# A gated delta-rule trunk: 512-column projections with a kept convolution edge, and the first tap on ScalarE

## The reference

```python
xn = rmsnorm(h, norm_g)
proj = xn @ w_in                                   # q, k, v, z (1024 columns each), two gate logits per head
qkv = silu(causal_depthwise_conv(proj[..., :3072], conv_w))   # 4 taps along the sequence, each channel by itself
q, k = l2norm(q) * 128 ** -0.5, l2norm(k)          # per head, 128 wide
o = chunked_delta_rule(q, k, v, beta, g)           # meta tokens as one chunk, the rest in chunks
h = h + (rmsnorm(o) * silu(z)) @ w_out
```

## Time and profile before

| | |
|---|---|
| median of three runs | 2801.99 us (2800.05 to 2802.21) |
| the profiled execution | 2798.55 us |
| its span, first to last instruction | 2796.6 us |
| mean granted TensorE clock | 0.958 |
| busy share: PE, DVE, ACT, POOL | 89%, 60%, 41%, 17% |
| `gated_deltanet` | from about 119 to about 1602 us |

### The profile page before, as it was taken

How to read it: one execution, slowest core, us unless ns; L and a number is a source line. 1 busy time by engine, 2 the same in 40 slices (tenths; PEclk the granted TensorE clock), 3 DMA queues, 4 the chain that set the end, 5 groups by cost and what they waited for, 6 DMA issues and landing times. The chain is left out here.

```text
span 2796.6 us, 50391 instructions
## 1 busy us (share of the span) xinstructions
PE 2498.3 (89%) x17193; PEld 2193.1 (78%) x17193; DVE 1671.3 (60%) x3872; ACT 1132.8 (41%) x3326; POOL 481.3 (17%) x377
## 2 busy tenths in 40 slices
PE   5568887899999999999999699999996999999997
PEld 4467777789998999999999468878885777777775
DVE  4367676777777777777777333333332666666664
ACT  4244454544444444444444244433331333333332
POOL 0144343310000000000000012100001333223331
PEclk9689999999999999999999689999997999999998
DMA  6664354544445444344453167743455222222221
GB/s 194 200 245 143 137 167 147 180 132 130 143 138 189 137 145 131 126 156 134 122 164 97 27 196 257 243 158 139 182 199 229 68 68 84 84 68 75 68 69 47
DMA packets 273813, 392.78 MB, mean 140 GB/s; under 512 B 79282, under 2 KB 187906, under 8 KB 273442
## 3 DMA queue, kind: packets, MB, share of 16 engines
q1 hardware_dynamic: 240066, 370.05, 39.6%
q10 hardware_dynamic: 33632, 21.26, 2.6%
HBM read 267.92 MB, written 123.31 MB: 140 GB/s over the span
## 5 line engine op out<-in xcount | busy, mean ns | idle before, releaser
L1227 PE MATMUL p_psp<-xg,p_whi 128*128 128x264 f32 x4096 | 842.4, 295 | 26.6 <-POOL p_wlo L1176 17.2
L1227 PEld LDWEIGHTS p_psp<-xg,p_whi 128*128 128x128 f32 x4096 | 655.5, 191 | 31.2 <-issue 21.9
L1227 PE MATMUL p_psp<-xg,p_wlo 128*128 128x264 f32 x2048 | 606.9, 296 | 0.0
L1227 PEld LDWEIGHTS p_psp<-xg,p_wlo 128*128 128x128 f32 x2048 | 391.6, 191 | 0.0
L981 DVE SCALAR_TENSOR_TENSOR p_acc<-p_proj,p_taps,p_acc 128x528 f32<-128x528 f32 x288 | 251.8, 874 | 5.4
L1822 PE MATMUL first_q<-first_w,p_o 128*128 128x512 f32 (+1 forms) x864 | 208.3, 401 | 17.0 <-DVE first_w L1786 17.0
L2364 PE MATMUL first_q<-first_w,p_hT 128*128 128x512 f32 x720 | 196.4, 413 | 13.4 <-DVE p_q L2250 13.0
L1822 PEld LDWEIGHTS first_q<-first_w,p_o 128*128 128x128 f32 (+1 forms) x864 | 157.4, 184 | 61.2 <-issue 17.0
L2364 PE MATMUL p_pso<-p_wo,p_oT 128*128 128x512 f32 x768 | 194.3, 404 | 7.9 <-DVE p_oT L2276 4.2
L862 ACT ACTIVATE p_sig<-p_sig 128x528 f32<-128x528 f32 x128 | 82.5, 645 | 293.1 <-DVE p_sig L983 293.1
L2364 PEld LDWEIGHTS p_pso<-p_wo,p_oT 128*128 128x128 f32 x768 | 143.7, 192 | 48.5 <-issue 16.1
(11 more groups left out here) (265 smaller groups left out, 4664.5 us busy)
## 6 DMA issues: line engine op xcount, KB each, us to landing
p_whi<-w_dram SPq DMA_DIRECT2D x92, 512.0 KB, 4.1
p_wlo<-w_dram SPq DMA_DIRECT2D x92, 512.0 KB, 5.2
raw<-w_a_in SPq DMA_DIRECT2D x36, 512.0 KB, 6.8
w_dram<-p_whi SPq DMA_DIRECT2D x34, 512.0 KB, 4.0
w_dram<-p_wlo SPq DMA_DIRECT2D x34, 512.0 KB, 5.3
p_o<-hT_dram SPq DMA_DIRECT2D x34, 512.0 KB, 4.7
hT_dram<-p_hT SPq DMA_DIRECT2D x32, 512.0 KB, 3.3
p_hT<-hT_dram SPq DMA_DIRECT2D x30, 512.0 KB, 4.0
```

Of the source, the lines that this page charges most:

```text
L1227: ins = nc.tensor.matmul(ps_p[half_][:, 0:HALF], (w_hi, w_lo)[i][:, f, kc * P:(kc + 1) * P], xg[:, g % 2, j, kc, half_ * HALF:(half_ + 1) ...
```

## The change

Items of the first group are projected as before, in halves, and ACT copies the last three columns of f0, f1 and f2 into a small tile `edge`, which has a place for 16 items. Items of later groups are projected in matmuls of 512 columns, without the 16 columns ahead; bank `ps_p[f % 2]` then holds a whole result. The item of the same head in the group before has left its last three columns in `edge`, and ACT copies them in front. `FILL` stays, with the slot's bounds halved. For later groups, ACT evacuates a whole result in the slot where the second half was evacuated, keeps its edge, and makes tap 0; DVE makes taps 1 to 3 and the maximum, 512 wide. The store of the last 16 columns in the first phase is gone, and group loads bring 512 columns.

```diff
-            def store_edge():
-                act.wait_ge(lo_ready, 2 * (TPG + 1))
-                for part in range(2):
-                    act.dma_start(xT_d[part][:, :, GW - META:GW], xg[:, 0, part, :, GW - META:GW].bitcast(f32)
-                                  ).then_inc(edge_out, 16)
...
-                    store_edge()
...
+        edge = sb("p2_edge", [P, 2 * H * 9])
...
-                    sp.dma_start(xg[:, g % 2, part].bitcast(f32), xT_d[part][:, :, g * TC:g * TC + GW]).then_inc(x_in, 16)
+                    sp.dma_start(xg[:, g % 2, part, :, 0:TC].bitcast(f32),
+                                 xT_d[part][:, :, META + g * TC:META + (g + 1) * TC]).then_inc(x_in, 16)
...
+            def evacuate_half(it, u):
...
+                if half_ and f < 3:
+                    nc.scalar.activation(edge_of(it, f), ps_p[1][:, HALF - 3:HALF], ACT.Copy)
                 nc.scalar.activation(proj[:, f % 2, 3 + half_ * HALF:3 + (half_ + 1) * HALF], ps_p[half_][:, 0:HALF],
                                      ACT.Copy).then_inc(proj_read, 1)
...
+            def evacuate(it, f):
+                buffer_free(it, f)
+                if f < 3:
+                    act.wait_ge(proj_read, 2 * NF * (it - H) + (2 * f + 2))
+                    nc.scalar.activation(proj[:, f % 2, META:META + 3], edge_of(it - H, f), ACT.Copy)
+                act.wait_ge(proj_ps, 2 * NF * it + (2 * f + 2))
+                nc.scalar.activation(proj[:, f % 2, 3 + META:3 + GW], ps_p[f % 2][:, 0:TC], ACT.Copy
+                                     ).then_inc(proj_read, 1 if f < 3 else 2)
+                if f < 3:
+                    nc.scalar.activation(edge_of(it, f), ps_p[f % 2][:, TC - 3:TC], ACT.Copy).then_inc(proj_read, 1)
+                    first_tap(it, f)
+
+            def first_tap(it, f):
+                act.wait_ge(taps_ready, it + 1)
+                act.wait_ge(silu_done, NF * it + (f - 1))
+                act.wait_ge(proj_read, 2 * NF * it + (2 * f + 2))
+                nc.scalar.activation(acc[:, f % 2, META:GW], proj[:, f % 2, META:GW], ACT.Copy,
+                                     scale=taps[:, 4 * f:4 * f + 1]).then_inc(tap_done, 1)
...
+                        elif u % 2:
+                            evacuate(item, u // 2)
...
-            def convolve(it, f, part):
+            def convolve(meta, it, f, part):
+                first = 0 if meta else META
+                cols = slice(first, GW)
+                p, a, v = proj[:, f % 2, first:], acc[:, f % 2, cols], sig[:, f % 2, cols]
+                width = GW - first
...
+                if part == 0 and not meta:
+                    return
...
-                    link(nc.vector.tensor_copy(taps[:], conv_w[:, bass.ds(head * 12, 12)]))
+                    nc.vector.tensor_copy(taps[:], conv_w[:, bass.ds(head * 12, 12)]).then_inc(taps_ready, 1)
+                    dve.wait_ge(taps_ready, p.item + 1)
...
+            def project(it, g, start, end):
+                for m in range(start, end):
+                    f, r = m // (3 * KC), m % (3 * KC)
+                    i, j, kc = split_parts(r // 3)[r % 3]
+                    if r == 0:
+                        weights_made(it, f)
+                        if isinstance(it, int) and it == H and f < 2:
+                            pe.wait_ge(proj_read, 2 * NF * it - (1 - f))
+                        else:
+                            pe.wait_ge(proj_read, 2 * NF * it + (2 * f - 2))
+                    ins = nc.tensor.matmul(ps_p[f % 2][:], (w_hi, w_lo)[i][:, f, kc * P:(kc + 1) * P],
+                                           xg[:, g % 2, j, kc, 0:TC], start=r == 0, stop=r == 3 * KC - 1)
+                    if r == 3 * KC - 1:
+                        ins.then_inc(proj_ps, 2)
...
+                        if g == 0:
+                            project_halves(it, slot.start, slot.end)
+                        else:
+                            project(it, g, slot.start // 2, slot.end // 2)
```

More of the change, by code:

```diff
@@ L464, in gated_deltanet @@
         tap_done = sem("p2_tap_done")
+        taps_ready = sem("p2_taps_ready")
         cleared = sem("p2_cleared")
@@ L627, in schedule @@
             for s, (back, f, parts) in TAPS.items():
-                base[s].taps += [(it - back, f, n) for n in parts if item[back]]
+                base[s].taps += [(item[back][0].meta, it - back, f, n) for n in parts if item[back]]
             for s, (back, f, parts) in SIGMOID.items():
-                base[s].sigmoid += [(it - back, f, n) for n in parts if item[back]]
+                base[s].sigmoid += [(item[back][0].meta, it - back, f, n) for n in parts if item[back]]
             for s, (back, f) in SILU.items():
@@ L633, in schedule @@
             for s, (back, u) in (EVACUATE_META if opening else EVACUATE).items():
-                base[s].evacuated += [(it - back, u)] if item[back] else []
+                base[s].evacuated += [(item[back][0].meta, it - back, u)] if item[back] else []
             for s, (ahead, f, part) in SPLIT.items():
@@ L843, in split_high, with buffer_free, edge_of @@
                 nc.scalar.activation(w_hi[:, f, cols], w_raw[:, slot, cols], ACT.Copy).then_inc(hi_ready, 1)
-            def evacuate(it, u):
+            def buffer_free(it, f):
+                if f % 2 == 0:
+                    act.wait_ge(conv_done, NF * it + (f - 1))
+                else:
+                    act.wait_ge(silu_done if f == 1 else conv_done, NF * it + (f - 1))
+            def edge_of(it, f):
+                place = it if isinstance(it, int) and it < 2 * H else it % (2 * H)
+                return edge[:, bass.ds(place * 9 + 3 * f, 3)]
+            def evacuate_half(it, u):
                 f, half_ = u // 2, u % 2
@@ L940, in step @@
                         stage_of(stage, q, index)
[L941 to L944, removed]
+                    for meta, item, u in slot.evacuated:
+                        if meta:
+                            evacuate_half(item, u)
+                        elif u % 2:
+                            evacuate(item, u // 2)
+                    for meta, item, f, part in slot.sigmoid:
+                        sigmoid(meta, item, f, part)
                     for item, f, part in slot.split:
@@ L1136, in step @@
                             silu(q, item, f, b)
-                    for item, f, part in slot.taps:
-                        convolve(item, f, part)
+                    for meta, item, f, part in slot.taps:
+                        convolve(meta, item, f, part)
                     for q, i in slot.rows:
@@ L1212, in _, with weights_made, project_halves @@
         def _(pe):
-            def project(it, g, start, end):
+            def weights_made(it, f):
+                if isinstance(it, int) and it <= H:
+                    pe.wait_ge(lo_ready, 2 * (NF * it + f + 1))
+                else:
+                    pe.wait_ge(split_in[f], 32 * (it - H))
+            def project_halves(it, start, end):
                 for m in range(start, end):
@@ L1359, in step @@
                             stage_of(stage, q, index, a, b)
-                        project(it, g, slot.start, slot.end)
+                        if g == 0:
+                            project_halves(it, slot.start, slot.end)
+                        else:
+                            project(it, g, slot.start // 2, slot.end // 2)
                 return step
```

28 lines of the change are left out of this document (10 added, 18 removed).

## The result

The changed kernel takes 2896.52 us (median of 4 runs, 2889.84 to 2897.54) against 2802.1 (4 runs, 2800.05 to 2804.01): a ratio of 1.0332, 95% interval 1.0319 to 1.0346. It is 94 us slower, where 3.5 us were predicted. The profiled execution spans 2895.2 us.

A forecast was written before the change was run, and what follows sets the result against it. A ring through PE, ACT and DVE was taken as the bound: steps +3.8, solve's return +1, first phase -1.3, total +3.5 us, so 2805 us. The range ran from 2784 to 2819 plus 3 us for rival 3's copies.

The forecast's parts named there:

- the sum per step: All changes to one later-group step together: +0.16 us with kg holding up e_last, -0.22 without that.
- (b): DVE's taps and triangular solve, up to PE's second "ks": narrower operations give -0.08 us, leaving +0.45.
- Rival 4: Something outside the other terms, such as DVE's solve gaining from ACT's shorter queue; no own time, chance 0.08.
- wrong, if it rises above 41.7: Sign against the forecast: a step period above 41.7 us would mean ACT late, in (a) or ahead of w.
- (a): f2's evacuation and first tap, now on ACT, ahead of DVE's tap 1: 1.48 us against 0.95, so +0.53.
- the ring: Chain of dependent work through PE, ACT and DVE in one later-group step, with a period of 41.3 us.
- (c): PE from second "ks" to third "out", then DVE's state update: 39 matmuls become 20, 0.18 us less, leaving +0.27.
- (d): f0's taps and ACT's sigmoid up to kT: evacuation gone -0.27 us, narrower passes -0.04, kT at -0.09.
- (e): Levels on PE and DVE to next f2's end: kg delays e_last, +0.30 us; fewer matmuls give -0.05.
- Rival 2: 512-column matmuls at their bare time, 0.2133 us, on the ring: 12 us less, 2793 us; chance 0.10.
- Rival 1: kg does not meet e_last in the later-group steps: -5.6 us in total, 2796 us; chance 0.24.
- Rival 3: ACT's chain ahead of f2's tap 1 is longer, +1.1 us: 14 us more, 2819 us; chance 0.22.

The follow-up runs named there:

- 40 places: Kernel before and changed kernel, each with 40 one-column VectorE memsets added in the first phase, shifting its later instructions: 2795.36 us and 2801.78 us.
- 97: Kernel before with 97 one-column VectorE memsets added in the first phase, work in the loops unchanged: 2793.74 us.
- the undone tap: Changed kernel with the later groups' first tap back on VectorE: 2797.81 us; with 30 one-column memsets added as well, 2791.6 us.
- 118 memsets: Kernel before with 118 one-column VectorE memsets added in the first phase, work in the loops unchanged: 2868.38 us.
- 102 memsets: Kernel before with 102 one-column VectorE memsets added in the first phase, work in the loops unchanged: 2867.77 us.

## Why the prediction was wrong

The step that failed is the sum per step, +0.16, as a sum of what instructions and waits cost. It took (b), "DVE works nearly without a gap", from a step of the kernel before, and let an edit of DVE's program change only the operations in it. The jump back lies in (b), and there the edit put 6.8 us, mostly 1.9 us more, and a slower PE, every other step. Rival 4, "something outside these", held the cause with no time of its own. The bound "wrong, if it rises above 41.7" did catch the case (45.6), but it named ScalarE for it, in (a) or ahead of w, and the ten gaps were at neither. What should have been read: the two gaps "remote" in the first group and the 50 fetches on the page, both there before.

With the code of both kernels moved by 40 places the rest of the prediction can be measured. One step of each, both with the jump back (without a miss) in it, DVE in order of time: state copy, f2's tap 1, first and last state update, kT, e_last, state copy. Before, 40 places:

```profile
1031.11 0.21 DVE L1081 COPY p_state<-p_states 128x128 f32 x1
...
1033.81 0.77 DVE L984 SCALAR_TENSOR_TENSOR p_acc<-p_proj,p_taps,p_acc 128x528 f32<-128x528 f32 x1
...
1044.74 0.35 DVE L1114 SCALAR_TENSOR_TENSOR p_state<-p_state,p_elast,p_psc 128x128 f32<-128x128 f32 x1
...
1057.67 0.35 DVE L1114 SCALAR_TENSOR_TENSOR p_state<-p_state,p_elast,p_psc 128x128 f32<-128x128 f32 x1
1058.62 0.69 DVE L1006 TENSOR_TENSOR p_kT<-p_acc,p_sig 128x512 f32<-128x512 f32 x1 [0.59 <-ACT p_sig L871]
...
1065.87 0.16 DVE L1053 COPY p_elast<-p_cur 128x4 f32<-128x4 f32 x1
...
1072.51 0.21 DVE L1081 COPY p_state<-p_states 128x128 f32 x1
```

Changed, 40 places:

```profile
1042.45 0.21 DVE L1112 COPY p_state<-p_states 128x128 f32 x1
...
1045.76 0.75 DVE L1014 SCALAR_TENSOR_TENSOR p_acc<-p_proj,p_taps,p_acc 128x512 f32<-128x512 f32 x1 [2.76 <-ACT p_acc L879]
...
1056.60 0.35 DVE L1145 SCALAR_TENSOR_TENSOR p_state<-p_state,p_elast,p_psc 128x128 f32<-128x128 f32 x1
...
1069.38 0.35 DVE L1145 SCALAR_TENSOR_TENSOR p_state<-p_state,p_elast,p_psc 128x128 f32<-128x128 f32 x1
1070.01 0.69 DVE L1036 TENSOR_TENSOR p_kT<-p_acc,p_sig 128x512 f32<-128x512 f32 x1 [0.28 <-ACT p_sig L893]
...
1077.20 0.49 DVE L1084 COPY p_elast<-p_cur 128x4 f32<-128x4 f32 x1
...
1084.11 0.21 DVE L1112 COPY p_state<-p_states 128x128 f32 x1
```

| place in the ring | before | changed | later by | predicted |
|---|---|---|---|---|
| f2's tap 1, (a) | 2.70 | 3.31 | +0.61 | +0.53 |
| first state update, (b) | 13.63 | 14.15 | +0.52 | +0.45 |
| last state update, (c) | 26.56 | 26.93 | +0.37 | +0.22 to +0.27 |
| kT, (d) | 27.51 | 27.56 | +0.05 | -0.09 |
| e_last, duration, (e) | 0.16 | 0.49 | +0.33 | +0.30 |
| next state copy | 41.40 | 41.66 | +0.26 | +0.16 |

- *(a)* was right in its parts. ACT in order of time in the changed kernel at 40 places, one step later: older edge, evacuation, new edge, tap.

```profile
1085.23 0.19 ACT L867 ACTIVATE p_proj<-p_edge 128x3 f32 x1
1085.85 0.60 ACT L869 ACTIVATE p_proj<-p_psp 128x512 f32<-128x512 f32 x1 [0.43 <-PE p_psp L1281]
1086.34 0.17 ACT L872 ACTIVATE p_edge<-p_psp 128x3 f32 x1
1086.62 0.72 ACT L879 ACTIVATE p_acc<-p_proj,p_taps 128x512 f32<-128x512 f32 x1
```

  Evacuation to the tap's end is 1.49 us, the sum said 1.45; the older edge is hidden, ACT waits 0.43 us for PE behind it.
- *(b)* -0.09 and *(d)* -0.32 were right to 0.02.
- *(c)* gave 0.15, not 0.18. 512-column matmuls are dearer than taken: PE in order of time, changed kernel, 15 from the first of these to the last, (1047.39 - 1043.91) / 15 = 0.232 us each, between the 0.2275 taken and the upper bound. Rival 2 is out with it.

```profile
1043.91 0.40 PE L1278 MATMUL p_psp<-xg,p_wlo 128*128 128x512 f32 x1
...
1047.39 0.39 PE L1278 MATMUL p_psp<-xg,p_wlo 128*128 128x512 f32 x1
```

- *(e)*, kg and e_last, was right in mechanism and size: e_r moved forward takes e_last back to 0.16 us and the period down by 41.68 - 41.35 = 0.33. Rival 1 is out. kg, to compare with the earlier trace rows, in the step above, on POOL:

```profile
1076.35 1.31 POOL L1221 TENSOR_TENSOR p_kg<-p_kT,p_er 128x512 f32<-128x512 f32 x1 [21.25 <-ACT p_er L904]
```

  It starts 6.34 us behind kT, where it was 5.13, and e_last (1077.20 to 1077.69) ends with it (1077.66), as the sum had it.

- Rival 3's mechanism, a longer chain on ScalarE, is there with 0.08 of the 0.57 a step that would make its 2819.
- Leaving f2's tap on VectorE was put at 0.32 us a step. The move back, with e_r early in both kernels, gained 9 us, 0.39 between like steps. So the rule of the Trainium skill that was weighed there ("ScalarE: Activation LUTs", Rules for kernel authors: multiplies to VectorE) was right for f2. For f0's and f1's together the runs speak against it, by about 8 of the 11 us above, with the open ends said there.
- The late landings of Xt cost PE's weight loads 2.1 us in three steps from 640 to 1560 us against 0.9 in one before, and with 40 places 2.8 in three against 4.7 in two: the 1 us taken for them can't be told from nothing. First phase and first group left the first state copy in its place, 629.2 against 628.9 us (a gain of 1.3 was taken, and the group's copies as hidden). That settles neither term: without a miss of DVE the kernel before has this copy at 619.2 us in one execution (40 places) and at 624.2 in another (97). ScalarE's two missed jumps there, about 1.2 us, were in no term.

So the work is 6 us dearer than before, about 1 of it ScalarE's two jumps, where 3.5 were predicted; 88 to 90 us are DVE's ten jumps back.

## What to carry to other kernels

Where a loop body is long on an engine, an edit that adds or removes instructions there, or anywhere ahead of it, can change the time by more than all the work in the edit; before believing a surprising loss or gain, compare the page's counts of instruction fetches and look for gaps that no instruction released where the body jumps back. To price an edit, run it with do-nothing instructions ahead of the loops, in both kernels, as many as it takes until neither trace has such a gap; here the undone tap seemed worth 99 us and was worth 10. And the fetches cost the kernel before 6 us as well, which 40 memsets got back.

## What the runs showed of the hardware

- A missed jump back of DVE's loop costs a gap of 3.3 to 11 us in DVE's own instructions; one of ScalarE's first-group loop took 2.5 us from the branch to the next instruction in place of 0.3. The gap is 3.3 to 3.6 us in all first-group loops that miss. It is 4.6 to 5.8 with a second of 2 us for 118 memsets (the loop starts 5 places ahead of a block's end and ends 16 into one), and 6.8 to 7.1 us with 102 (21 places, 0). What sets the one or the other isn't settled. The DMA share differs between the two kinds of place. Windows from the jump on, as at the top, of the kernel before in the first group (gap 3.35 us, one fetch of q14 in it) and of the changed one in a later group (6.77 us, two fetches); the share, last but one, is 0.11 and 0.82:

```profile
329.50:332.90 3.40, 0.00 (x0) 0.00 (x0) 0.05 (x2) 0.73 (x2) 2.59 (x3) 1.00 0.11 45
1094.70:1098.00 3.30, 0.16 (x1) 0.00 (x0) 0.00 (x0) 0.34 (x1) 0.00 (x0) 1.00 0.82 314
```

  That a fetch takes longer beside such transfers is a guess; no run changed them.
- A loop of 262 instructions missed where one of 278 did not: the length within three blocks (384) decides nothing, the place does.
- The Trainium skill ("Runtime: NRT & Kernel Launch", Instruction fetch mechanics) says that code is fetched ahead in sequence, and that a taken branch to a target outside the window held stalls for a fetch. The ten gaps and five fetches for each agree with that. Its sizes for an engine like DVE, blocks of 16 KiB, 256 instructions, and two of them held, don't fit here: q14's fetches are of 8192 bytes, and the kernel before with 102 memsets, 939-1216, would touch two such blocks, counted from place 64, and miss nothing; counted from 192, the changed kernel's 827-1088 would. The measurement decides: blocks of 128, of which a loop can use three without a fetch.
- A jump back that hits isn't free: the steps with it in them take 41.40 us and those without it 40.87 (kernel before, 40 places); the first r waits 0.79 us in the ones and 0.28 in the others.
